# Attention's steps set between pieces of the projections and quarters of the output product

## The reference, cut to what matters

```
def stick_breaking_mixer(xn, w_in, q_gain, k_gain, w_out):
    q, k, v = jnp.split(xn @ w_in, 3, axis=-1)
    q = rms_norm_2(q.reshape(b, s, SB_HEADS, SB_DH), q_gain)...transpose(0, 2, 1, 3)
    k = rms_norm_2(k.reshape(b, s, SB_HEADS, SB_DH), k_gain)...transpose(0, 2, 1, 3)
    v = v.reshape(b, s, SB_HEADS, SB_DH)...transpose(0, 2, 1, 3)
    for b0 in range(0, s, SB_BLOCK):                       # two blocks of 128 rows
        kend = b0 + SB_BLOCK
        z = einsum('bhqd,bhkd->bhqk', q[:, :, b0:kend], k[:, :, :kend]) * scale
        mask = s_idx[None, :] < t_idx[:, None]
        log_1mb = where(mask, log_sigmoid(-z), 0.0)
        log_w = log_sigmoid(z) + cumsum(log_1mb, axis=3, reverse=True) - log_1mb
        a = where(mask, exp(log_w), 0.0)
        outs.append(einsum('bhqk,bhkd->bhqd', a, v[:, :, :kend]))
    return concatenate(outs, axis=2)... @ w_out
```

## Time and profile before

| | |
|---|---|
| median of 3 runs | 2007.58 us (2006.42 to 2007.86) |
| the profiled execution, its own time | 2005.12 us |
| its span | 2003.8 us |
| TensorE busy | 1950.4 us, 97% |
| VectorE busy | 1320.5 us, 66% |
| ScalarE busy | 1056.9 us, 53% |
| chain that ended last | PE 87%, DVE 6%, ACT 4%, DMA 2%, issue 2% |
| mean granted clock of TensorE | 0.989 |

### The profile page before, as it was taken

One profiled execution on the slowest core, in us unless ns is written; L12 is line 12 of the kernel. 1 busy time (PEld: TensorE's weight loads), 2 busy tenths in 40 slices (PEclk: granted clock), 3 DMA queues, 4 the chain that ended last, 5 costly groups with the idle time before them and its releaser, 6 DMA issues.

```text
span 2003.8 us, 26354 instructions
## 1 busy us (share of the span) xinstructions
PE 1950.4 (97%) x10828; PEld 1648.7 (82%) x10828; DVE 1320.5 (66%) x1682; ACT 1056.9 (53%) x1337; POOL 7.3 (0%) x8
## 2 busy tenths in 40 slices
PE   9899999999999999999999999999999999999998
PEld 4788896778888888888987888897788898888886
DVE  3876776787875566656795666656666675667654
ACT  4337764777754556444565444555544453555442
POOL 0000000000000000000000000000000000000000
PEclk9999999999999999999998999999999999999999
DMA  9851125899945445555411655541355555346551
GB/s 346 294 174 63 64 89 204 303 317 318 306 151 178 138 156 175 186 197 181 149 50 65 210 188 191 170 156 65 138 191 188 189 189 173 122 151 207 175 204 74
DMA packets 230563, 354.86 MB, mean 177 GB/s; under 512 B 7690, under 2 KB 180523, under 8 KB 230188
## 3 DMA queue, kind: packets, MB, share of 16 engines
q1 hardware_dynamic: 229714, 352.90, 51.9%
q10 hardware_dynamic: 730, 0.27, 0.1%
HBM read 352.10 MB, written 1.05 MB: 176 GB/s over the span
## 4 chain that ended last, share of the span: by engine, by line
PE 87%; DVE 6%; ACT 4%; DMA 2%; issue 2%; SPq 0%; DVEq 0%; ACTq 0%
PE bank L597 13%; PE bank L599 13%; PE bank L598 13%; PE bank L640 11%; PE bank L619 6%; PE bank L621 6%; PE bank L620 6%; PE bank L638 5%; PE bank L1217 2%; DVE wlo L1919 2%; ACT whi L1364 1%; PE bank L967 1%; DMA raw<-in_hg_w_in 1%; PE bank L643 1%; PE bank L731 1%
## 5 line engine op out<-in xcount | busy, mean ns | idle before, releaser
L1919 DVE TENSOR_TENSOR wlo<-raw,whi 128x2048 fp32r<-128x2048 f32 x282 | 644.5, 2291 | 218.9 <-ACT whi L1364 217.6
L1364 ACT CAST whi<-raw 128x2048 fp32r<-128x2048 f32 x282 | 536.4, 1909 | 158.3 <-PE bank L599 118.9
L640 PE MATMUL bank<-HH,whi 128*128 128x512 f32 x1024 | 365.5, 397 | 0.5
L619 PE MATMUL bank<-HH,whi 128*128 128x256 f32 (+1 forms) x1024 | 315.8, 308 | 13.1 <-ACT ARENA L1503 4.0
L597 PE MATMUL bank<-whi,YH 128*128 128x512 f32 x816 | 321.7, 394 | 7.0 <-DVE YL L2506 2.5
L599 PE MATMUL bank<-whi,YL 128*128 128x512 f32 x816 | 319.5, 392 | 0.0
L598 PE MATMUL bank<-wlo,YH 128*128 128x512 f32 x816 | 319.5, 392 | 0.0
L620 PE MATMUL bank<-HL,whi 128*128 128x256 f32 (+1 forms) x1024 | 307.1, 300 | 0.0
L621 PE MATMUL bank<-HH,wlo 128*128 128x256 f32 (+1 forms) x1024 | 307.0, 300 | 0.0
L638 PE MATMUL bank<-HH,wlo 128*128 128x256 f32 x896 | 252.2, 281 | 0.1
L640 PEld LDWEIGHTS bank<-HH,whi 128*128 128x128 f32 x1024 | 192.1, 188 | 44.4 <-issue 1.6
(11 more groups left out here) (383 smaller groups left out, 2178.8 us busy)
## 6 DMA issues: line engine op xcount, KB each, us to landing
raw<-in_ffn_w SPq DMA_DIRECT2D x128, 1024.0 KB, 5.3
raw<-in_ret_w_in SPq DMA_DIRECT2D x48, 1024.0 KB, 5.2
ARENA<-in_w_mod SPq DMA_DIRECT2D x21, 1024.0 KB, 10.4
raw<-in_hg_w_in SPq DMA_DIRECT2D x20, 1024.0 KB, 7.4
raw<-in_ret_w_out SPq DMA_DIRECT2D x16, 1024.0 KB, 4.9
raw<-in_moe_w_gate SPq DMA_DIRECT2D x26, 512.0 KB, 4.8
raw<-in_moe_w_up SPq DMA_DIRECT2D x26, 512.0 KB, 5.7
raw<-in_moe_w_down SPq DMA_DIRECT2D x12, 1024.0 KB, 7.3
```

The costliest lines, as they stand in the source:

```text
L619: pe.matmul(ps, w[0][:, k, c], ah, start=begin, stop=False, skip_group_check=True)
L640: x = pe.matmul(bank[bs[m]][:, :], w[0][:, k, c], HW[:, k, :], start=k == 0, stop=k == 7, skip_group_check=True)
L1364: ac.copy(whi[i % NS][:, :], raw[place[i]][:, :]).then_inc(*whi_("w", i))
L1919: ve.tensor_tensor(wlo[i % NS][:, :], raw[place[i]][:, :], f32(whi[i % NS][:, :]), SUB).then_inc(*wlv("w", i))
```

## The change

`proj_a` gets `between`, up to four calls that are made behind its four groups of six matmuls. `proj_b` has such a place already: before its third k, that is after 12 of its 48 matmuls. In the tiles 5, 6 and 7 step 2n-9 is now issued there, and step 2n-8 alone behind the tile; ScalarE and VectorE have step 2n-9 right behind the tile's `take()`. `back(0)` comes behind step 7, and its groups are followed by step 8, step 9, spread(3) and step 10. Step 11 follows, then `back(1)` with steps 12, 13 and 14 behind its first three groups, step 15, `back(2)` with steps 16, 17 and 18 in the same way, and `back(3)`. On ScalarE and VectorE step 7 moves behind scales(3). The heads' four groups of four use the banks 3, 7, 6, 7 instead of 7, 3, 7, 6, and the group of two banks begins at scores of head 10 (13 before) and turn of head 8 (11 before). The takes behind steps 11, 13 and 15 stay.

```diff
-            def proj_a(stage, acts, k0, begin, end):
+            def proj_a(stage, acts, k0, begin, end, between=()):
...
                         if end and q < 3:
                             x.then_inc(*prj("acc", stage, q))
+                        if 2 * h + m < len(between):
+                            between[2 * h + m]()
                 x.then_inc(*prj("item", i))
...
                 def scores(h):
-                    b = banks.next(pe, group if h < 13 else late_group, "sb_scores", h)
+                    b = banks.next(pe, group if h < 10 else late_group, "sb_scores", h)
...
                 def turn(h):
                     pe.wait_ge(*vec.at("sb_a", h))
-                    b = banks.next(pe, group if h < 11 else late_group, "sb_turn", h)
+                    b = banks.next(pe, group if h < 8 else late_group, "sb_turn", h)
...
                     if h % 4 == 0:
-                        banks.hold(pe, (7, 3, 7, 6)[q], "sb_y", q)
-                    y = bank[(7, 3, 7, 6)[q]]
+                        banks.hold(pe, (3, 7, 6, 7)[q], "sb_y", q)
+                    y = bank[(3, 7, 6, 7)[q]]
...
-                def back(j):
+                def back(j, between=()):
                     pe.wait_ge(*vlo.at("sb_y", j))
-                    proj_a("sb", Y8, 2 * j, j == 0, j == 3)
+                    proj_a("sb", Y8, 2 * j, j == 0, j == 3, between)
 
                 for n in range(8):
-                    proj_b(("sb", n), group=group)
+                    proj_b(("sb", n), group=group, between=(lambda: step(2 * n - 9)) if n > 4 else None)
                     if n:
                         squares(n - 1)
                     if n >= 3 and n % 2:
                         spread((n - 3) // 2)
                     if n >= 4:
                         step(2 * n - 8)
-                        step(2 * n - 7)
                 squares(7)
-                step(8)
-                step(9)
-                spread(3)
-                step(10)
+                step(7)
+                back(0, (lambda: step(8), lambda: step(9), lambda: spread(3), lambda: step(10)))
                 step(11)
-                for j in range(3):
-                    back(j)
-                    step(12 + 2 * j)
-                    step(13 + 2 * j)
-                step(18)
+                back(1, (lambda: step(12), lambda: step(13), lambda: step(14)))
+                step(15)
+                back(2, (lambda: step(16), lambda: step(17), lambda: step(18)))
                 back(3)
...
                 for n in range(8):
                     take()
+                    if n > 4:
+                        step(2 * n - 9)
                     head(n)
                     if n >= 2 and n % 2 == 0:
                         scales((n - 2) // 2)
                     if n >= 4:
                         step(2 * n - 8)
-                        step(2 * n - 7)
                 scales(3)
-                for n in range(8, 19):
+                for n in range(7, 19):
                     step(n)
                     if n in (11, 13, 15):
                         take()
...
                 for n in range(8):
                     take()
+                    if n > 4:
+                        step(2 * n - 9)
                     if n:
                         mean_squares(n - 1)
...
                     if n >= 4:
                         step(2 * n - 8)
-                        step(2 * n - 7)
                 mean_squares(7)
                 scales(3)
-                for n in range(8, 18):
+                for n in range(7, 18):
                     if n == 10:
                         scaled(3)
                     step(n)
```

## The result

The change made the kernel slower: 2016.38 us (median of 5 runs, 2014.72 to 2017.52) against 2006.42 (5 runs, 2002.73 to 2007.86). The ratio is 1.0061, with an interval of 1.0048 to 1.0075, that is 10 to 15 us. The forecast was 2012.8, +5.2 us, and a range up to 2016.3. The direction was right; the size was about half, and the time lies just outside the range. The forecast was added to 2007.58, the median of three runs; against that the change costs 8.8 us, against the median of five 10.0.

A forecast was written before the change was run, and what follows sets the result against it. TensorE, busy for 97% of the span, was taken as the bound. Added work +2.6, vanished stalls -6.8 and new stalls +9.4 gave +5.2 us on the median of 2007.58, so 2012.8 us, range 2007.8 to 2016.3.

The forecast's parts named there:

- The work added: TensorE's queue: split projections 0.6, parted scores 0.3, more entries and exits of output quarters 1.7; together +2.6 us.
- the eight stalls that go: Attention stage: seven turns waiting for VectorE and one wait for low(3) vanish, covered by quarters or pieces; -6.8 us.
- Quarters set apart: Output tiles: six matmuls standing alone cost 1.57 us, including 0.19 for entering and leaving.
- (4): Steps 10 and 11 remain back to back: a stall of 0.35 us, plus 0.1 for low(1).
- The new stalls: Walking the three queues from 1331.08 gives new waits of TensorE throughout the stage, summing to 9.4 us.
- point (1): Tile 5: take before step delays Square and Identity, so spread(1) waits 1.1 us for projection 5's own bank.
- squares(5) and (6): Behind tiles 6 and 7: squares get the projection's own bank and wait for Square and Identity, 1.35 us each.
- turn(15): After step 15: VectorE's wlo and scan make it ready +7.7 after turn(13), TensorE comes at +5.8; stall 1.9 us.
- The 1.4 before `back(0)`: back(0) waits for low(0), as scales(3) now precedes step 7 on ScalarE and VectorE; stall 1.4 us.
- The sum at equal clock: Whole stage: +2.6 for work, -6.8 for old stalls, +9.4 for new ones, giving +5.2 us at the same clock.
- the one on the clock: Attention stage: the old low-clock place goes, turn(15) brings about as likely another; one stretch costs 3.0 us.
- Case C: One low-clock stretch more than before, at squares or back(0) as well as turn(15); +8.2 us, 2015.8, chance 0.1.

The follow-up runs named there:

- e3: Changed kernel with squares, spread(0) to spread(2) and scores of heads 0 to 7 in idle banks 0, 1 and 2; 2006.03 us, 1.0004 of before.
- e6: Changed kernel with five dense matmuls nobody reads put into one wait, ahead of squares(6) behind tile 7; 2012.16 us, 1.0034 of before.
- e4: Changed kernel with dense matmuls nobody reads put into the waits ahead of spread(1), squares(5), squares(6) and back(0); 2010.08 us, 1.0023 of before.
- e7: Kernel before with six dense matmuls nobody reads put into its longest wait of the stage, that of turn(3); 2003.14 us, 0.9990 of before.
- e2: Kernel before with only the output's half of the change and the new banks, tiles as before; 2009.61 us, 1.0019 of before.
- e1: Changed kernel with only the tiles' half kept, output and banks as in the kernel before; 2014.94 us, 1.0053 of before.

## Why the prediction was right, and where it was wrong

**The work added, +2.6, and the eight stalls that go, -6.8.** Right as far as the runs separate them. Quarters set apart took 1.55 (1413.83 to 1415.38, in `back(2)`) to 1.60 us (1405.53 to 1407.13, in `back(1)`), where 1.57 was reckoned, and `back(3)` waits for nothing. The 2.6 as a whole was not measured by itself. Of the eight old waits one is left, that of the pair of steps 10 and 11, as forecast under (4).

**The new stalls, 9.4.** The order of the queues was as walked. ScalarE and VectorE of the changed kernel in tile 5, point (1):

```profile
1333.32 1.89 ACT L1362 CAST whi<-raw 128x2048 fp32r<-128x2048 f32 x1
1338.22 0.52 ACT L1856 ACTIVATE ARENA<-ARENA 128x384 f32<-128x384 f32 x1 [3.01 <-DVE ARENA L2719]
...
1339.54 0.59 ACT L1840 ACTIVATE ARENA<-bank 128x512 f32<-128x512 f32 x1
```

```profile
1335.24 2.29 DVE L1918 TENSOR_TENSOR wlo<-raw,whi 128x2048 fp32r<-128x2048 f32 x1 [2.98 <-ACT whi L1362]
1337.45 0.73 DVE L2719 SCALAR_TENSOR_TENSOR ARENA<-bank,SM,ARENA 128x128 f32<-128x128 f32 x2
```

The execution ran 0.6 us ahead of the other one at the first scores; with that, the cast (reckoned 1333.9), wlo (1335.9), masked(1) (1338.1) and the end of Identity (1340.8) all fall within 0.1 us. The waits: spread(1) 1.0 in the view (reckoned 1.1), squares(5) and (6) 1.3 and 1.2 (1.35), turn(11) and turn(13) and turn(9) the other 1.6 of L1290's 3.5 (1.75 with the scores' waits apart), turn(15) 1.9 (1.9). Two small ones are not in the list of waits: the last matmuls of their quarters start at 1402.22 and 1410.53, and scores(13) and scores(15) 0.46 and 0.45 later, 0.15 more than the usual 0.31 (reckoned 0.15 and 0.2). The 1.4 before `back(0)` is hidden in this execution and stands as 1.3 in e3 and e6. turn(15) came 7.65 us after turn(13) (1412.56 to 1420.21; reckoned 7.7).

**The sum at equal clock, +5.2.** Two kernels without any low clock in the stage give it: e4, which is the changed kernel with its waits filled, 93.7 us, and e7, which is the kernel before with one wait filled, 88.2. The difference is 5.5. The filling costs next to nothing in e4: squares(6) starts at 1367.39, and the Identity that it waits for ends at 1367.34.

**The step that failed** is the one on the clock: "the waits of 1.15 and 1.45 brought none", and so "from one such stretch of 3.0 us to about as likely another". I read from the kernel before that a wait of 1.4 us is harmless, and put the danger above all at the 1.9 of turn(15). In this kernel three waits of 1.0 to 1.3 us each were followed by a fall, and the 1.9 by none in the profiled execution. The low clock cost 101.7 - 93.7 = 8.0 us for 20.5 us of it, 0.39 us for each, where before it cost 91.2 - 88.2 = 3.0 for 6.8, which is 0.44. (The 8.0 is net of the 1.3 before `back(0)`, which the long stretch hides; an estimate with it is 9.3, or 0.45 for each.) So the parts are +5.5 for work and waits and +5.0 for the clock, together the 10.5 of the stage. Case C had the mechanism, at squares, with a chance of 0.1 and a price of 3.0 for one more stretch; the stretch behind tile 7 alone was twice as long as the one of before.

The reading of the old fall was also loose. The prediction has it follow the wait of 1.8 us, but the turn that ends this wait starts after the fall at 1356.2:

```profile
1356.41 0.90 PE L1287 MATMUL bank<-CST,ARENA 128*128 128x128 f32 x3 [1.78 <-DVE ARENA L2734]
```

So there the clock fell within the wait, 0.2 us before its end (and so in e2, at 1361.25 with the turn at 1361.45), while in the changed kernel it fell 1.2 to 1.7 us behind shorter waits. The length of the wait just before was no measure of the danger.

That the changed kernel has more low clock is not seen in the profiled executions alone: the granted clock of the timed runs is 0.986 on average over five of the changed kernel, and 0.990 over 26 of the kernel before.

**Rules and rows.** The Trainium skill ("ScalarE: Activation LUTs", What ACT_TABLE_LOAD costs) adds a drain to each table load, by which the wait before `back(0)` would have been 2.8 us. e3 and e6 show 1.3, so the row was the better guide. The Trainium skill ("TensorE: Matmul & The Clock Gate", The HAM clock gate) has the clock fall after a stretch in which TensorE was idle. The trace does not bear this out as the prediction read it: the clock fell at 1341.5 though TensorE had been busy for 2.47 of 3.5 us, with no wait longer than 1.03.

**What stays open.** Why the waits beside squares bring a fall, and the 1.3 before `back(0)` (e6, e3) none, isn't settled. In the profiles no stretch came among the tiles where these waits were taken out or filled (e3, e4), but what else TensorE does near them was not varied by itself. The 1.9 before turn(15) was followed by a stretch in e3 and e6 (1.8 and 1.3 us later) and by none in e2, e4 and the changed kernel; nothing here separates chance from cause in that.

## What to carry to other kernels

A short wait of TensorE has two prices: its own length, and the low clock that can follow it among small matmuls, which here cost nearly as much (5.0 us) as all the work and waits that the change added (5.5). Whoever interleaves work should walk the ring of banks and the in-order queues of the other engines again: a ring that was long enough gives a step its neighbour's bank, and a cast that lay behind a long tile stands ahead of a head. Each of these was mended by moving a few lines, and the interleaving with these mends was 0.4% faster than the kernel before (0.24 to 0.51).

## What the hardware showed that I had not expected

- The long stretches of low clock stood over small work: 13.7 us in the changed kernel, until the first quarter of `back(0)`, and 20.5 in e1, where more steps come in a row. With one wait filled (e6) the first of them did not come. TensorE had no idle time in either, so no wait is needed to keep one up.
- Matmuls that nobody reads can pay: 19 of them, some 0.23 us each, set into waits, took 6 to 8 us off the changed kernel (e4), and 6 of them 1.7 off the kernel before (e7, by the medians; the interval is 0.2 to 3.8).
- The runs spread with the clock: the 26 runs of the kernel before that were measured together lie between 2002.94 and 2009.78, with mean clocks from 0.992 down to 0.987, the slower ones as a rule at the lower clock.
